# Second input projection and window attention: reads and tiles in another order, value products in pairs, key work divided, first output low parts earlier

## The reference

```python
def mixer_window_attention(q, k, v, gate, sink, bias, mask):
    ...                       # 8 blocks of 128 queries, 8 query heads of 64, 2 key/value heads
    s = jnp.einsum('bnqkgd,bnskd->bnkgqs', q, kb).astype(jnp.float32) * (HEAD_DIM ** -0.5)
    s = jnp.where(mask[None, :, None, None], s + bias, NEG_INF)
    m = jnp.maximum(jnp.max(s, axis=-1, keepdims=True), sk)
    p = jnp.exp(s - m)
    p = p / (jnp.sum(p, axis=-1, keepdims=True) + jnp.exp(sk - m))
    o = jnp.einsum('bnkgqs,bnskd->bnqkgd', p.astype(vb.dtype), vb)
    return o.reshape(bsz, seq, W_C) * jax.nn.silu(gate)
```

## Time and profile before

| | |
|---|---|
| median of three runs | 1657.49 us (1654.9 to 1658.04) |
| the profiled execution | 1655.6 us, of which the span (first to last instruction) is 1653.7 us |
| granted clock | 0.998 |
| PE busy | 1616.9 us, 98% |
| DVE busy | 1157.4 us, 70% |
| POOL busy | 701.2 us, 42% |
| ACT busy | 624.3 us, 38% |

### The profile page before, as it was taken

One profiled execution on the slowest core, in us unless ns is written; L12 is line 12 of the kernel. 1 busy time (PEld: TensorE's weight loads), 2 busy tenths in 40 slices (PEclk: granted clock), 3 DMA queues, 4 the chain that ended last, 5 costly groups with the idle time before them and its releaser, 6 DMA issues.

```text
span 1653.7 us, 21507 instructions
## 1 busy us (share of the span) xinstructions
PE 1616.9 (98%) x7846; PEld 1322.0 (80%) x7846; DVE 1157.4 (70%) x1704; ACT 624.3 (38%) x987; POOL 701.2 (42%) x387
## 2 busy tenths in 40 slices
PE   9999999999999999999999999999999999999997
PEld 5888887888877888888887778887778888878785
DVE  6341898963498777777767656886977993597466
ACT  6221433421265444444443222264561021278214
POOL 2444111145514333223327687753555545442552
PEclk9999999999999999999999999999999999999999
DMA  5511010141623443444359986231201111110112
GB/s 197 92 47 48 29 39 26 31 153 59 219 85 140 153 153 140 151 155 154 152 201 356 396 324 259 109 141 63 64 13 47 42 51 51 47 44 1 31 34 102
DMA packets 54568, 190.34 MB, mean 115 GB/s; under 512 B 5857, under 2 KB 7842, under 8 KB 53834
## 3 DMA queue, kind: packets, MB, share of 16 engines
q1 hardware_dynamic: 49362, 171.66, 28.5%
q10 hardware_dynamic: 5112, 17.44, 3.6%
HBM read 134.02 MB, written 55.05 MB: 114 GB/s over the span
## 4 chain that ended last, share of the span: by engine, by line
PE 56%; DVE 6%; DMA 2%; issue 2%; SPq 1%; ACT 1%; POOL 1%; ACTq 0%; POOLq 0%; DVEq 0%
PE G L804 15%; PE U L1069 11%; PE G L1069 10%; PE U L1107 5%; PE G L1107 4%; PE G L1143 4%; PE G L1241 2%; PE U L1329 1%; PE G L1318 1%; SPq L515 1%; DMA fraw<-in_weights 1%; DMA raw<-in_weights 1%; DMA hid_spill<-hst 1%; DVE h L2432 1%; PE U L1241 1%
## 5 line engine op out<-in xcount | busy, mean ns | idle before, releaser
L622 POOL TENSOR_SCALAR w_hi<-raw 128x1024 fp32r<-128x1024 f32 x48 | 142.2, 2962 | 275.4 <-PE G L804 215.3
L804 PE MATMUL G<-B_hi,w_hi 128*128 128x512 f32 x480 | 149.8, 393 | 2.6 <-DVE B_lo L2044 2.4
L804 PE MATMUL G<-B_lo,w_hi 128*128 128x512 f32 x480 | 148.0, 389 | 0.0
L804 PE MATMUL G<-B_hi,w_lo 128*128 128x512 f32 x480 | 147.8, 389 | 0.0
L666 POOL TENSOR_TENSOR S<-fraw 128x512 f32<-128x512 f32 x33 | 47.1, 1428 | 222.3 <-DVE ring_lo L2327 195.3
L804 PE MATMUL G<-A_hi,w_hi 128*128 128x512 f32 x432 | 138.9, 403 | 0.0
L804 PE MATMUL G<-A_lo,w_hi 128*128 128x512 f32 x432 | 133.5, 390 | 0.0
L804 PE MATMUL G<-A_hi,w_lo 128*128 128x512 f32 x432 | 133.2, 389 | 0.0
L624 POOL TENSOR_TENSOR w_lo<-raw,w_hi 128x1024 fp32r<-128x1024 f32 x48 | 127.8, 2662 | 4.0
L1069 PE MATMUL G<-X_lo,ring_hi 128*128 128x512 f32 x308 | 120.3, 391 | 2.3 <-DVE X_lo L2322 2.3
L1069 PE MATMUL G<-X_hi,ring_hi 128*128 128x512 f32 x308 | 120.1, 390 | 1.8 <-DVE ring_lo L2327 1.2
(11 more groups left out here) (419 smaller groups left out, 3845.4 us busy)
## 6 DMA issues: line engine op xcount, KB each, us to landing
raw<-in_weights SPq DMA_DIRECT2D x72, 512.0 KB, 3.5
hid_spill<-hst SPq DMA_DIRECT2D x72, 512.0 KB, 2.6
fraw<-in_weights SPq DMA_DIRECT2D x66, 512.0 KB, 4.5
Dc<-hid_spill SPq DMA_DIRECT2D x56, 512.0 KB, 12.9
Dc<-hid_spill ACTq DMA_DIRECT2D x14, 512.0 KB, 7.9
h<-in_x_t SPq DMA_DIRECT2D x8, 512.0 KB, 7.9
h_spill<-h SPq DMA_DIRECT2D x8, 512.0 KB, 6.4
pj_spill<-pj_out SPq DMA_DIRECT2D x8, 512.0 KB, 2.6
```

What stands on the lines that cost most here:

```text
L622: pool.tensor_scalar(hi, raw[:, u, :], 1.0, None, ALU.mult).then_inc(w_hi_done, 1)
L804: mm = pe.matmul(G[g][:, b * HT:(b + 1) * HT], w, x[:, k, b * HT:(b + 1) * HT], start=s0, stop=s1)
```

## The change

- `half_rows(N1, 0)` stands two input tiles later in the last piece, `half_sums(N1, 1)` one tile later in `quad(0)`. At k = 0 `quad(0)` does high and low products of outputs 0 to 2 and then those of output 3. DVE reads the last piece ahead of the norm of tiles 2 and 3 and takes these one by one; ACT moves a square behind the third `normed_hi`, and in the second half reads `quad_half(0)` and `(1)` after one tile in place of two.
- `pT` has eight head slots in place of four (so `qs1` and `spread_inv` lie elsewhere), and `values` takes four heads in one visit: 256 moving columns in place of 128, two visits a block in place of four.
- `inverse_rows` is a transpose in place of a product with the identity.
- High parts of the first keys are made by ACT in place of DVE; the low parts of the second key head by POOL in place of DVE; `queries(1, 1)` stands ahead of the spatial gating. POOL splits the first two output slots together, after its last query part.
- In blocks 6 and 7 ACT makes all of `exps(7)` at once, DVE copies the transposed heads of block 6, and ACT those of block 7.
- DVE makes `B_lo[1]` after block 6, and the first output product takes k in the order 1, 0, 2, ..., 7.

Removed and added lines only, eight leading blanks cut; the removed lines of `quad` stand in the listing above:

```diff
@@ -293,15 +293,15 @@
-qs = [at("qs0", 52, [P, 2, 4, P], F32R), at("qs1", 112, [P, 2, 4, P], F32R)]
+qs = [at("qs0", 52, [P, 2, 4, P], F32R), at("qs1", 124, [P, 2, 4, P], F32R)]
-pT = at("pT", 104, [P, 4, 3, P])
-spread_inv = at("spread_inv", 110, [P, 4, 2, HD])
+pT = at("pT", 104, [P, HEADS2, 3, P])
+spread_inv = at("spread_inv", 116, [P, 4, 2, HD])
...
@@ -755,18 +755,26 @@
+    def keys_lo(e):
+        own = rows_of(1)[0]
+        pool.nop(nofuse=True)
+        pool.tensor_tensor(k_lo[1][rows_of(1)[e], :], ck[own, :], f(k_hi[1][own, :]), ALU.subtract).then_inc(k_lo_done[1], 1)
+    pool.wait_ge(b_read, 1)
+    pool.wait_ge(k_hi_done, 6)
+    keys_lo(0), keys_lo(1)
-    pool.wait_ge(pt_done, HEADS2)
-    pool.wait_ge(qs_done, 8)
-    split(1, S_OUT2, bufs[1])
-    pool.wait_ge(w_split, S_OUT2 + 1)
+    pool.wait_ge(pt_done, HEADS2)
+    split(1, S_OUT2, bufs[1])
+    split(0, S_OUT2 + 1, bufs[0], wait=False)
...
@@ -776,7 +784,7 @@
-    for s, dst in ((1, bufs[0]), (2, bufs[1]), (3, bufs[0]), (4, bufs[1]), (5, bufs[0])):
+    for s, dst in ((2, bufs[1]), (3, bufs[0]), (4, bufs[1]), (5, bufs[0])):
...
@@ -808,19 +816,19 @@
-    def gemm(u, s, a, g, hi, lo, op=None, free=True, before=None, after={}):
+    def gemm(u, s, a, g, hi, lo, op=None, free=True, before=None, after={}, order=range(KT)):
-        for k in range(KT):
+        for i, k in enumerate(order):
-                pe.wait_ge(op_lo, op + k + 1)
-            three(u, k, KT, g, hi, lo, k, k == 0, k == KT - 1,
-                  first=(k == 0 and not (isinstance(s, int) and s == 0)),
-                  last=acc_done if k == KT - 1 else after.get(k))
+                pe.wait_ge(op_lo, op + i + 1)
+            three(u, k, KT, g, hi, lo, k, i == 0, i == KT - 1,
+                  first=(i == 0 and not (isinstance(s, int) and s == 0)),
+                  last=acc_done if i == KT - 1 else after.get(k))
...
@@ -1192,7 +1200,7 @@
-    at_piece = {6: {0: lambda: half_sums(N1, 0, acc2)}, 7: {0: lambda: half_rows(N1, 0)}}
+    at_piece = {6: {0: lambda: half_sums(N1, 0, acc2)}, 7: {2: lambda: half_rows(N1, 0)}}
...
@@ -1222,30 +1230,42 @@
+    def quad_hi(n, k, j):
+        if k == 0:
+            quad_free(n, j)
+        wh, wl = (t[:, k * P:(k + 1) * P] for t in quad_w[j])
+        x = B_hi[:, k, hs(n)]
+        mm = pe.matmul(quad_bank[n][j], wh, x, start=(k == 0), stop=False)
+        if n == 0 and k == 0:
+            mm.then_inc(w_used, 1)
+        pe.matmul(quad_bank[n][j], wl, x, start=False, stop=False)
+    def quad_lo(n, k, j):
+        mm = pe.matmul(quad_bank[n][j], quad_w[j][0][:, k * P:(k + 1) * P], B_lo[:, k, hs(n)], start=False, stop=(k == KT - 1))
+        if k == KT - 1:
+            mm.then_inc(acc_done if n else pc_made, 1)
+            parts = ((0, 1, 2, 3),)
+            if n == 0 and k == 0:
+                parts = (0, 1, 2), (3,)
+            elif n and k == KT - 1:
+                parts = ((2, 3, 0, 1),)
+            for part in parts:
+                for j in part:
+                    quad_hi(n, k, j)
+                pe.wait_ge(op_lo, 3 * KT + KT * n + k + 1)
+                for j in part:
+                    quad_lo(n, k, j)
+    quad(0, {5: lambda: half_sums(N1, 1, acc2), 7: lambda: half_rows(N1, 1)})
...
@@ -1319,15 +1339,16 @@
-    def values(n, par, j, nkb, kb0):
-        pe.wait_ge(pT_done, n * HEADS2 + 2 * j + 2)
-        if j == 0 and n >= 1:
+    def values(n, par, half, nkb, kb0):
+        pe.wait_ge(pT_done, n * HEADS2 + 4 * half + 4)
+        if half == 0 and n >= 1:
-                mm = pe.matmul(U[HD * g:HD * g + HD, 2 + par, j * P:(j + 1) * P], Vt[:, kb0 + kb, HD * g:HD * g + HD],
-                               pT[:, (2 * j + g) % 4, kb, :], start=(kb == 0), stop=(kb == nkb - 1))
+                two = pT[:, 4 * half:4 * half + 4, kb, :].rearrange("p (j g) n -> p j g n", g=2)[:, :, g, :]
+                mm = pe.matmul(U[HD * g:HD * g + HD, 2 + par, 2 * half * P:2 * (half + 1) * P].rearrange("p (j n) -> p j n", j=2),
+                               Vt[:, kb0 + kb, HD * g:HD * g + HD], two, start=(kb == 0), stop=(kb == nkb - 1))
...
@@ -1335,8 +1356,7 @@
-            mm = pe.matmul(U[:, 3 - n % 2, j * P:(j + 1) * P], spread_inv[:, j, :, :].rearrange("p a n -> p (a n)"), ident[:, :],
-                           start=True, stop=True)
+            mm = pe.transpose(U[:, 3 - n % 2, j * P:(j + 1) * P], spread_inv[:, j, :, :].rearrange("p a n -> p (a n)"), ident[:, :])
...
@@ -1346,9 +1366,9 @@
-                values(n - 1, (n - 1) % 2, 3, *left)
-            if e % 2 and e >= 3:
-                values(n, n % 2, e // 2 - 1, nkb, kb0)
+                values(n - 1, (n - 1) % 2, 1, *left)
+            if e == 5:
+                values(n, n % 2, 0, nkb, kb0)
...
@@ -1375,24 +1395,25 @@
+            pe.wait_ge(k_hi_done, 8)
-        if e % 2:
-            values(0, 0, e // 2, 2, 0)
+        if e % 4 == 3:
+            values(0, 0, e // 4, 2, 0)
-    values(7, 1, 3, 2, 6)
-    gemm(1, S_OUT2, C_OUT2 // 2, 1, B_hi, B_lo, op=3 * KT + X2)
+    values(7, 1, 1, 2, 6)
+    gemm(1, S_OUT2, C_OUT2 // 2, 1, B_hi, B_lo, op=3 * KT + X2, order=(1, 0, *range(2, KT)))
...
@@ -1831,8 +1852,8 @@
-    normed_hi(0, 0), piece_square(6, 0), normed_hi(1, 0), piece_gate(7), piece_square(6, 1)
-    normed_hi(2, 0), normed_hi(3, 0), piece_square(7, 0), normed_hi(4, 0), piece_square(7, 1), normed_hi(5, 0)
+    normed_hi(0, 0), piece_square(6, 0), normed_hi(1, 0), piece_gate(7)
+    normed_hi(2, 0), piece_square(6, 1), normed_hi(3, 0), piece_square(7, 0), normed_hi(4, 0), piece_square(7, 1), normed_hi(5, 0)
...
@@ -1848,9 +1869,9 @@
-    normed_hi(0, 1), normed_hi(1, 1)
+    normed_hi(0, 1)
-    normed_hi(2, 1), normed_hi(3, 1)
+    normed_hi(1, 1), normed_hi(2, 1), normed_hi(3, 1)
...
@@ -1904,6 +1925,11 @@
+    act.wait_ge(acc_free[1], (C_IN2 + 16) // 2 + 1)
+    for g in range(2):
+        own, other = rows_of(g)
+        for to in (own, other):
+            act.activation(k0_hi[g][to, :], ck[own, 0:BAND], ACT.Copy).then_inc(k_hi_done, 1)
...
@@ -1917,10 +1943,10 @@
-    for g in range(2):
-        own, other = rows_of(g)
-        for to in (own, other):
-            act.activation(k_hi[g][to, :], ck[own, :], ACT.Copy).then_inc(k_hi_done, 1)
+    for e in range(2):
+        for g in range(2):
+            own = rows_of(g)[0]
+            act.activation(k_hi[g][rows_of(g)[e], :], ck[own, :], ACT.Copy).then_inc(k_hi_done, 1)
...
@@ -1934,9 +1960,9 @@
-        if not (isinstance(n, int) and n * HEADS2 + e < 4):
-            act.wait_ge(pv_done, n * 4 + e // 2 - 1)
-        act.activation(pT[:, e % 4, 0:nkb, :].rearrange("p k n -> p (k n)"),
+        if not (isinstance(n, int) and n == 0):
+            act.wait_ge(pv_done, 2 * n + e // 4 - 1)
+        act.activation(pT[:, e, 0:nkb, :].rearrange("p k n -> p (k n)"),
...
@@ -1961,8 +1987,10 @@
-    turned_block(5, 1, 3, BAND), turned_block(6, 0, 3, 2 * P)
+    turned_block(5, 1, 3, BAND)
+    for hd in range(HEADS2):
+        exps(7, 1, hd, 2 * P)
+    act.wait_ge(pT_done, 7 * HEADS2)
...
@@ -2626,8 +2654,7 @@
-    piece_added(6, p6), normed(N1, 0, 2, 3)
-    piece_read(7), piece_centre(6), sq1(6, 0)
+    piece_added(6, p6), piece_read(7), normed(N1, 0, 2), piece_centre(6), normed(N1, 0, 3), sq1(6, 0)
...
@@ -2723,13 +2750,13 @@
-    def keys_lo(g, e):
-        own = rows_of(g)[0]
+    def keys_lo(e):
+        own = rows_of(0)[0]
-            dve.wait_ge(k_hi_done, 2 * g + 2)
+            dve.wait_ge(k_hi_done, 5)
-        dve.tensor_tensor(k_lo[g][rows_of(g)[e], :], ck[own, :], f(k_hi[g][own, :]), ALU.subtract).then_inc(k_lo_done[g], 1)
+        dve.tensor_tensor(k_lo[0][rows_of(0)[e], :], ck[own, :], f(k_hi[0][own, :]), ALU.subtract).then_inc(k_lo_done[0], 1)
...
@@ -2757,7 +2784,7 @@
-        dve.wait_ge(pv_done, 4 * n + 4)
+        dve.wait_ge(pv_done, 2 * n + 2)
...
@@ -2765,12 +2792,11 @@
-    for g in range(2):
-        own, other = rows_of(g)
-        for to in (own, other):
-            tick(dve.tensor_copy(k0_hi[g][to, :], ck[own, 0:BAND]))
-    tick.wait()
+    dve.wait_ge(k_hi_done, 4)
+    dve.wait_ge(cs_done, 2)
+    dve.wait_ge(w_split, S_OUT2)
+    queries(1, 1)
...
@@ -2782,8 +2808,6 @@
-    dve.wait_ge(w_split, S_OUT2)
-    queries(1, 1)
...
@@ -2801,27 +2825,43 @@
-            keys_lo(0, 0)
+            keys_lo(0)
-    shifts(0, 0), keys_lo(0, 1), queries(2, 0), keys_lo(1, 0)
+    shifts(0, 0), queries(2, 0), keys_lo(1)
-        if hd == HEADS2 // 2:
-            keys_lo(1, 1)
-    step(5, 1, 2 * P), step(6, 0), step(7, 1)
+    step(5, 1, 2 * P)
+    def turned_w(n, e, nkb):
+        dve.wait_ge(pt_done, n * HEADS2 + e + 1)
+        dve.wait_ge(pv_done, 2 * n + e // 4 - 1)
+        dve.tensor_copy(pT[:, e, 0:nkb, :].rearrange("p k n -> p (k n)"), G[0][:, e % 2 * HT:e % 2 * HT + nkb * P]).then_inc(pT_done, 1)
+    def operand_low(k):
+        low(B_hi, B_lo, k, k, branch(k), 3 * KT + X2 + k)
+    dve.wait_ge(pT_done, 6 * HEADS2)
+    turned_w(6, 0, 3), turned_w(6, 1, 3)
+    denominators(6, 0)
```

(41 more changed lines are left out.)

## The result

The kernel after takes 1646.45 us (median of 4 runs, 1645.08 to 1647.95), the kernel before 1657.76 (4 runs, 1654.9 to 1658.55). The ratio is 0.9933, its 95% interval 0.9921 to 0.9945: 11.3 us faster, between 9.1 and 13.1. 1643.0 had been forecast, with a range from 1638.5 to 1648; the median is outside the forecast's own range of 1641 to 1645.

A forecast was written before the change was run, and what follows sets the result against it. TensorE, busy in 98% of the span, was taken as the bound. 3.2 + 3.3 + 4.5 + 3.4 = 14.4 us off the profiled 1655.6, plus 1.9 to the median: 1643.1 (forecast 1643.0), range 1638.5 to 1648, its own 1641 to 1645.

The forecast's parts named there:

- A: Second projection: earlier read of the last piece and reordered tiles remove TensorE waits; 3.2 us gained, between 0.5 and 3.7.
- rival 2: Second projection: ACT's and DVE's late tiles move as much as PE, gain given back; A 0.5, time 1645.8; chance 0.1.
- B: Attention up to the start of block 2: cheaper visits and inverses, a wait for a maximum gone; 3.3 us, between 1 and 5.
- The 0.3 taken off for `queries(1, 1)`: Before block 0's scores: POOL's query part runs beside DVE's gating products, delaying keys; 0.3 us lost, can be 1.
- C: Attention blocks 2 to 5: each 1.12 us shorter, 9.24 us a block; 4.5 us gained, floor 1.5, top 5.5.
- The price per block: Attention blocks 2 to 5: two visits saving 0.32 each and the inverse 0.48, 1.12 us a block.
- the moves priced at nothing: POOL's output splits run in blocks 4 and 5, later slot loads, eight `pT` slots: no cost; splits running over, at most 2 us.
- rival 1: Attention: DVE becomes the bound, blocks 2 to 5 at 9.8, blocks 0 and 1 lose 1 us; time 1646.3; chance 0.17.
- D: Blocks 6 and 7 save 1.6 us, waits in the first output product 1.75; 3.4 us in sum, between 0.5 and 5.5.
- 0.6 of waits for DVE's copies: Blocks 6 and 7: TensorE waits 0.6 us for DVE's copies of heads, part of the 13.1 us forecast there.
- rival 3: Blocks 6 and 7: DVE's chain sets 14.5 us, half of the 1.75 stays; D 1.1, time 1645.4; chance 0.13.
- The sign I had named as refuting: Forecast wrong if attention, from block 0's scores to the output product, is not 8 us shorter or more.

The follow-up runs named there:

- small_sum: The kernel after, with GpSimd adding only 8 of the 512 columns of piece 6 to the sum; 1646.2 us, ratio 0.9932.
- inverse_only: The kernel before, with one edit: inverse denominators reach PSUM by transposes in place of float32 products; 1654.04 us, ratio 0.9978.
- narrow_products: The kernel after, with value products of the wide visits 128 columns wide, two for each of 256; 1647.09 us, ratio 0.9938.
- splits_spread: The kernel after, with GpSimd's two output-weight splits cut into four operations, one in each of blocks 1 to 4; 1646.9 us, ratio 0.9934.
- act_copies: The kernel after, with ScalarE copying all eight heads of block 6 and VectorE none; 1646.29 us, ratio 0.9938.
- shared_copies: The kernel after, with block 6's heads 0 to 3 copied by VectorE (then gate(5), denominators), 4 to 7 by ScalarE; 1646.64 us, ratio 0.9937.

## Why the prediction came out as it did

The time lies in the range, but the steps add up to 5.5 us too much, and a part of the hit is luck. Stages give 8.9 us, the medians 11.3: with 8.9 the forecast's base of 1657.5 would have come to 1648.6, just outside the range.

**A, 3.2 forecast, 1.75 measured.** The mechanism was right and so was every number up to k = 1 (2.7; the waits for `gs` and `half_rows` gone). The failed sentence is "DVE's total work is the same, so all its later steps keep their times within 0.2 us". The work was the same, but its last piece moved beside GpSimd's subtraction and addition and took 1.6 us more (1.29 and 1.67 against 0.7 each). Of the 1.9 us lost between k = 1 and `quad(1)`, small_sum, which shortens only the second of the two, gives 0.9 back; no run takes the other apart. The 1.75 lies halfway to rival 2's 0.5: the late tiles did move, for a reason that the rival doesn't name. I had the row for it, an addition that ended 0.5 us after GpSimd's subtraction, and used it for the attention only. `yb` gave more than the 0.5 forecast: its wait of 0.55 and the refilling around it were 0.87.

**B, 3.3 forecast, 3.3 measured.** The wait of 1.3 us for the maximum went. The 0.3 taken off for `queries(1, 1)` was 0.48, at the start of the scores. Where before waited 0.67 for a copy `pT` and 0.55 for the spread inverses, after waits 0.74 and 0.17. No run has the moved key parts alone, so of the rest only the sum is measured, and that it meets the forecast may be luck.

**C, 4.5 forecast, 2.7 measured.** The price per block was right: 1.12 forecast, 1.06 in blocks 2 and 3, of which 0.46 is the inverse (inverse_only) and 0.3 each visit less, whatever its width (narrow_products). The failed step is the one among the moves priced at nothing: the splits "run in blocks 4 and 5" and were priced only for running over. They did not run over, they held VectorE's small operations, as rival 1 said with its chance of 0.17 and spread over too many blocks. splits_spread returns 1.14 us. Of what is then still missing, most lies in block 5, which I had priced like the others: it took 9.55 before and takes 8.89 in splits_spread, 0.66 less and not 1.12. The Trainium skill ("SBUF — State Buffer", section Who interferes with whom) had been cited for that rival; its rule for two SBUF inputs agrees with the 1.29 and 1.67 above. It says that one side fully blocks where VectorE is in a two-port mode, which a copy or `tensor_scalar` can enter; `nm`, ending 0.04 us after GpSimd's low part, agrees. Beside GpSimd's `w_hi` the same `nm` took 0.99 and ended 1.7 us before it (1509.35 and 1511.06), which is no full block, and there the measurement decides.

**D, 3.4 forecast, 1.1 measured.** The output product gave 2.65, not 1.75: where its two inner waits of 1.76 went, their refilling went too, and a stall too short to be listed. That the earlier splits did it is argued from VectorE's shorter low parts; no run has them alone. But blocks 6 and 7 became 1.5 longer in place of 1.6 shorter. The failed term is "0.6 of waits for DVE's copies" in the 13.1, for 16.18 measured: the waits for copies are 2.60, of which 1.44 for VectorE's. The rest of the 3.1 us is not taken apart; TensorE counts as busy for 13.57, refilling included, where I had 11.1 of work. No wait for `inverse_rows(7)` is listed, for which I had 1.4. I summed TensorE's work and each engine's, and left out that with two places in PSUM a transpose waits for the copy two heads back. The narrow visits had hidden that, and pairing them took the cover away. The total of 1.1 is rival 3's to the digit, by chance: the rival has 14.5 for the blocks and half of the 1.75 lost in the product. Nor is its mechanism, a chain of VectorE, the one: with VectorE relieved (act_copies, shared_copies) the tail stays above 16.4. Without the pairing, the transposed inverse alone had made it 15.64.

The sign I had named as refuting, an attention less than 8 us shorter, did come: it is 5.0 us shorter (88.89 to 83.91).

What stays open is the difference between stages (8.9) and medians (11.3, interval from 9.1). The record points at the clock. The 49 executions of the kernel before that were timed beside the experiments average 1655.3 us at a granted clock of 0.998, 1656.8 at 0.997, 1658.4 at 0.996 and 1659.8 at 0.995. After's four have 0.997 twice and 0.999 twice, and the two at 0.997 average 1647.3: 9.5 less than before at the same clock, near the 8.9 of the stages, if from two executions. The rest would then be time at the lower clock outside the stages. Whether the change itself brings the higher clock is not shown.
